# First part of a fused network kernel: the mixer's first weights ahead of the ninth modulation chunk, later chunks set wider, spatial half 0 ahead of half 1

## The reference, cut to what matters

```
for i in range(2):
    m = (silu(c) @ w_mod[i] + b_mod[i]).reshape(6, 1024)       # shifts, scales, gates
    h = x * (1 + s1) + sh1
    mix = chunk_mlp(h, ...) if i == 0 else gla_mixer(h, ...)
    x = layer_norm(DN_ALPHA * x + g1 * mix, ln_g[i, 0], ln_b[i, 0])
    x = layer_norm(DN_ALPHA * x + g2 * peer_ffn(x * (1 + s2) + sh2, ...), ...)

chunk_mlp:  u, v = split(gelu(h @ w_in));  v = layer_norm(v)
            s = W_s @ v (8 heads of 128 channels, over 128 positions) + b_s
            return (u * s) @ w_out
peer_ffn:   q = h @ w_q;  scores = q @ keys;  16 picks for each of 8 heads and row,
            out = sum_k weight_k * gelu(u_table[pick] . h) * v_table[pick]
```

## Time and profile before

| | |
|---|---|
| Three runs | 3691.73, 3691.20, 3690.06 us; median 3691.2 |
| Span of the profiled execution | 3684.9 us |
| Median less that span | 6.3 us |
| TensorE clock granted over the span | 0.972 |
| PE, DVE, ACT, POOL busy | 88%, 68%, 48%, 23% |
| DMA read from HBM | 1159.79 MB, 315 GB/s over the span |

### The profile page before, as it was taken

The page is one execution under the profiler, slowest core; times in us unless marked ns, Lnnn a source line. Parts: engine busy times, 40 slices in busy tenths (PEclk is TensorE's granted clock), DMA queues, the critical chain, the costliest instruction groups (busy, mean ns, idle before and its releaser), DMA issues. The chain is left out here.

```text
span 3684.9 us, 38027 instructions
## 1 busy us (share of the span) xinstructions
PE 3244.8 (88%) x12780; PEld 2023.3 (55%) x12780; DVE 2523.6 (68%) x5106; ACT 1769.7 (48%) x3833; POOL 863.8 (23%) x778
## 2 busy tenths in 40 slices
PE   6878888887798889888887878789999999999998
PEld 3444444442354434446322222279878988988896
DVE  2577778867777787657677677567665657666655
ACT  2334445444554565554444444355464545555453
POOL 0024444444443444410444444300000000000000
PEclk8989999999999999999999999999999999999999
DMA  9979999999999999972999999956655655565553
GB/s 398 373 292 418 418 419 405 419 418 416 418 392 417 419 420 418 419 276 93 410 421 421 421 419 420 418 177 182 184 184 166 186 176 173 166 185 197 157 188 131
DMA packets 280468, 1163.47 MB, mean 316 GB/s; under 512 B 31144, under 2 KB 33704, under 8 KB 175824
## 3 DMA queue, kind: packets, MB, share of 16 engines
q0 software_dynamic: 110592, 805.36, 52.8%
q1 hardware_dynamic: 169296, 355.45, 29.1%
q10 hardware_dynamic: 384, 0.23, 0.0%
HBM read 1159.79 MB, written 1.15 MB: 315 GB/s over the span
## 5 line engine op out<-in xcount | busy, mean ns | idle before, releaser
L86 PE MATMUL psum<-rows,diag 128*128 128x512 f32 x3072 | 1491.5, 622 | 315.9 <-ACT diag L2164 315.0
L2120 DVE CUSTOM_DVE_ANT_0 rows<-rows,h 128x1024 f32<-128x1024 f32 x768 | 938.9, 1224 | 495.9 <-DMA rows<-in_p_uv,place 493.7
L86 PEld LDWEIGHTS psum<-rows,diag 128*128 128x128 f32 x3072 | 559.2, 194 | 1160.8 <-ACT diag L2164 665.8
L2016 POOL DMA_INDIRECT rows<-in_p_uv,place x768 | 859.8, 1120 | 1416.5 <-PE psum L86 1113.8
L2864 DVE TENSOR_TENSOR weights_low<-landing,weights_high 128x1024 fp32r<-128x1024 f32 x400 | 487.0, 1222 | 369.1 <-ACT weights_high L2811 368.0
L2811 ACT CAST weights_high<-landing 128x1024 fp32r<-128x1024 f32 x400 | 417.7, 1049 | 544.9 <-PE psum L86 362.8
L2151 ACT ACTIVATE acted<-dots 128x1 f32<-128x1 f32 x768 | 155.2, 202 | 927.4 <-DVE dots L2120 925.6
L86 PE MATMUL psum<-weights_high,hT_high 128*128 128x512 f32 x832 | 352.9, 424 | 14.5 <-DVE h L694 6.8
L2164 ACT ACTIVATE diag<-ident,weight 128x128 f32<-128x128 f32 x768 | 308.5, 402 | 70.4 <-ACT weight L2157 0.4
L86 PE MATMUL psum<-weights_high,hT_low 128*128 128x512 f32 x832 | 325.8, 392 | 0.0
L86 PE MATMUL psum<-weights_low,hT_high 128*128 128x512 f32 x832 | 325.7, 391 | 0.0
(11 more groups left out here) (431 smaller groups left out, 3875.0 us busy)
## 6 DMA issues: line engine op xcount, KB each, us to landing
landing<-in_w_in SPq DMA_DIRECT2D x192, 512.0 KB, 3.9
landing<-in_w_ff SPq DMA_DIRECT2D x128, 512.0 KB, 4.3
landing<-in_w_mod SPq DMA_DIRECT2D x48, 1024.0 KB, 8.7
landing<-in_a_w_in SPq DMA_DIRECT2D x64, 256.0 KB, 7.4
landing<-in_w_br SPq DMA_DIRECT2D x32, 512.0 KB, 4.3
rows<-in_p_uv,place POOLq DMA_INDIRECT x768, 15.3
lat_landing<-in_b_w_in SPq DMA_DIRECT2D x48, 256.0 KB, 7.4
landing<-in_a_w_out SPq DMA_DIRECT2D x32, 256.0 KB, 7.5
```

Source lines behind the costliest of these rows:

```text
L86: return k.nc.tensor.matmul(out, lhsT, rhs, start=first, stop=last)
L2016: k.nc.gpsimd.indirect_dma_start(rows[:, n % ROW_RING, :], None, k.given["p_uv"], bass.IndirectOffsetOnAxis(place[:, g % 4, c:c + 1], 0))\
L2120: V.tensor_tensor_reduce(u, u, token, 1.0, 0.0, ALU.mult, ALU.add, dots[:, g % 4, c:c + 1]).then_inc(dots_done, 1)
```

## The change

The chunks of the modulation lose the even spacing of 3.5 slots. The mixer's first four blocks are asked for at slot -10, ahead of chunk 8. Rows for v's norm, `ws` and the layer norm are asked for four blocks later. Spatial half 0 and its turns stand 8 slots earlier, half 1 5.5 and 3 slots earlier, blocks 32 to 39 3 to 5 slots and 40 to 47 3 slots earlier. The last store of modulation rows stands at slot 152, and POOL waits for the stores at gather 6 and not at gather 0. No transfer and no arithmetic is added or removed.

```
-AHEAD, MOD_SPREAD = -12, 3.5
+AHEAD = -12
 condition:
-    SLOTS = [AHEAD + n for n in range(DB)] + [1 + MOD_SPREAD * n for n in range(CHUNKS - DB)]
+    SLOTS = [AHEAD + n for n in range(DB)] + [1, 3.5, 6.5] + [11 + 4.1 * n for n in range(13)] \
+        + [66 + 3.4 * n for n in range(12)] + [106 + 1.4 * n for n in range(7)] + [117.5, 121, 122, 126, 130]
 stores:
-            yield SLOTS[DB * q + 7] + 4
+            yield SLOTS[DB * q + 7] + (4 if q + 1 < QUARTERS else 22)
 first_mix:
-    SLOTS = [8 + 2 * n for n in range(32)] + [77, 79, 81, 83, 86, 88, 90, 92] + [94 + 2 * n for n in range(8)] \
+    SLOTS = [8 + 2 * n for n in range(32)] + [72, 74, 76, 78, 83, 85, 87, 89] + [91 + 2 * n for n in range(8)] \
         + [123 + 2 * n for n in range(16)]
-        return SLOTS[p] - 15.5
+        return AHEAD + 2 if s == 0 and p < LANDING else SLOTS[p] - 15.5
 sp_rows:
-        yield load_slot(s, 4) + 0.5
+        yield load_slot(s, 4 if s == 1 else 8) + 0.5
-            yield load_slot(s, 6) + 0.5
+            yield load_slot(s, 10) + 0.5
-            yield load_slot(s, 12) + 0.5
+            yield load_slot(s, 16) + 0.5
-    TURNS_Y = ((0, 0, 72), (1, 0, 72), (0, 1, 82), (1, 1, 82))
+    TURNS_Y = ((0, 0, 64), (1, 0, 64), (0, 1, 79), (1, 1, 79))
-    SPATIAL = ((0, 0, 66), (1, 0, 66), (0, 1, 76), (1, 1, 76))
+    SPATIAL = ((0, 0, 58), (1, 0, 58), (0, 1, 70.5), (1, 1, 70.5))
 wait_rows_free (POOL):
             if n == 0:
                 conditioned.wait_used(pool)
+            if n == 6:
                 conditioned.wait_stored(pool, conditioned.quarters)
```

## The result

The changed kernel took 3697.8 us (median of 11 runs), the kernel before 3690.1 in the 11 runs beside it; ratio 1.0019, 95% interval 1.0011 to 1.0027. Forecast were 3689.4 us and a range to 3696.

What follows compares the result with a forecast made beforehand. Transfers were taken as the bound from the first gather on, so only the first score's time counted: 204.09 - 202.3 = 1.8 us gained, 3691.2 - 1.8 = 3689.4 us, range 3681 to 3696.

Steps and rivals of the forecast that it cites:

- The bound, and that it passes on: From the first gather on, transfers bound the kernel, so an earlier first gather passes through nearly one to one.
- The start: First blocks on PE: early requests let block 0 start near 44.6 us, 6.3 us earlier.
- The list of landings: Chunks and blocks up to the third store land one behind another, chunks 2.49 us apart, a block 0.63 us at 417 GB/s.
- The store wait: SP's wait for the third store: queue drains, SP goes on at 117.0, a DMA hole of about 2.7 us.
- Blocks 36 to 47: On PE, 23.7 us plus some 0.7 for a slow restart; block 47 done at 159.8, 8.3 us earlier.
- The stage behind: Block 47 to block 48: chunks still owed hold block 51 until 180.7; block 48 starts at 183.4, 0.4 us earlier.
- The ring limit: Chunk n + 6 is asked for only when chunk n is used; chunk 41 lands at 163.3, a hole about 3 us.
- The queries: Block 48 to first score: 17.1 us with three chunks fewer, plus 1.8 for PE's slow clock; score at 202.3.
- Sum: First score at 202.3 instead of 204.09, so 1.8 us off the whole: 3689.4 us.
- the store wait decides: Rival, chance 0.13: SP goes on at 123.5 behind the third store, score at 208.8, 4.7 us lost, 3695.9 us.
- full queue: Rival, chance 0.22: no holes before the gathers, DMA at 417 GB/s throughout, 10 us gained, 8 with one hole left, 3682.
- 6.3 us around the span: Whole kernel: the runs stand 6.3 us above the profiled execution's span of 3684.9, giving 3691.2 us before the change.

Runs made afterwards that it cites:

- u_early: The changed kernel with blocks 0 to 3 and the row loads asked for at their old places; 3696.5 us, ratio 1.0020 to the kernel before.
- u_spacing: The changed kernel with the modulation chunks evenly 3.5 slots apart again; 3688.0 us, ratio 0.9998 to the kernel before.
- u_wait: The changed kernel with the loads of g_row and m_rows at slot 74 instead of 65; 3691.4 us, ratio 1.0006 to the kernel before.
- t_only: The changed kernel with blocks 48 to 51 asked for 6.5 slots earlier, ahead of chunks 42 to 47; 3689.9 us, ratio 0.9998 to the kernel before.
- s_store: u_spacing with the third quarter's store at slot 64.5 instead of 57.5; 3691.8 us, ratio 1.0004 to the kernel before.
- c_old: The changed kernel with its context half (among the gathers) in the order of before; 3695.6 us, ratio 1.0018 to the kernel before.

## Why the prediction was wrong, point by point

- **The bound, and that it passes on**: right. The stage of gathers was as long as before to 1 us.
- **The start**: block 0 at 43.5 (44.6 predicted); no worth of it shows in u_early. But block 30 didn't land near 108: ACT got it at 112.59, after waiting 3.06 us for it. The list of landings let DMA run full until the store; DMA moved 320 GB/s at 100 to 120 us, not 417. This is the step that failed first. The gates and block 31's low part followed at about the predicted distance, so block 35 was asked for at 117.2 (112.8) and the store went out at 117.6 (113.5): 4.1 us late. "Block 31 done at 119.2" was wrong too, it was done at 125.7, outside the stated bounds; but PE later stood idle for 6.9 us ahead of block 36, so that delay isn't on the chain. Why block 30 landed late is open: in u_spacing DMA moved 410 to 417 GB/s from 110 to 130 us, and block 35 was asked for no earlier (117.5).
- **The store wait**: the mechanism was there, its size too small: SP paused 5.2 us (3.5) and went on at 122.8, not at 117.0. From there to block 36 it took 22.3 us (18.4), a second mis-sized term: the three row loads were priced at 417 GB/s, and behind them DMA moved 229 and 219 GB/s in the windows 124 to 126 and 126 to 128 us. Together with the late store that makes block 36 9.7 us late (4.1 + 1.7 + 3.9). u_wait shows what the wait cost: 4.8 to 8.2 us at block 36.
- **Blocks 36 to 47**: 25.3 us (24.4 predicted), end at 170.5 (159.8). Everything up to here is 10.7 us.
- **The stage behind**: right in kind. The ring limit, block 51 behind chunks 42 to 47 and the second turn behind block 51 came as described; 26.5 us for 23.6. The prediction so named the debt that t_only then removed, and still forecast a gain, because it had block 47 early enough to pay for it.
- **The queries**: 18.05 us to the first score (18.9), at the slow clock at first, as the earlier trace rows had shown behind an idle time. From the first score to gather 0 it was 12.15 us, as predicted.
- **Sum**: the first score was predicted at 202.3 and came at 214.96: 9.7 + 0.9 + 2.9 - 0.8 = 12.7 us late. The rule "a loss once block 47 ends later than 161.6" held, and so did the sign of being wrong, gather 0 after 217. The rival *the store wait decides* was the case, with 13%. Its time for SP, 123.5, was met within 0.7 us by luck: it put the store at 113.5 with 10.0 us behind it, and the store came 4.1 us later with 5.2 us behind it. Its price of 4.7 us at the score was short by 6.2 through the terms behind it (3.9, 0.9 and 2.9, less 0.7 and 0.8).
- **Two slips** that change nothing: the earlier trace rows has four requests between store and loads, two chunks and two blocks, and not three; and 167.6 + 5 + 1 in *full queue* is 173.6, not 173.9.
- **The range** ended at that rival's price, 3696, so it had no room for the rival being dearer than its price. The 7.7 us measured are just over the 7.4 that the prediction took as the least that tells; slower by more than that had got 0.07.
- **6.3 us around the span**: wrong. The profiled execution of the changed kernel took 3700.57 us at a span of 3698.8; 1.8 us lie around it. If as much lay around the span of before, that execution took 3686.7 us and was 3 to 4 us quicker than the median. The forecast isn't touched by it, since the 6.3 cancel in the sum.
- **The pool wait** at 0 and the context half at 0: right.

## What to carry to other kernels

When transfers are moved behind a stage, look which later transfer stands in line behind them and which engine's queue waits for that one: here 256 KB (block 51) held back some 8 us of PE through ACT's and DVE's order, and asking for it 6.5 slots earlier undid it. Keep a store and the load that waits for it apart by requests that others need. A forecast that lists landings one behind the other is a lower bound: check that someone asks for each of them in time. Before a single part of a change is priced from one profile, look whether the two profiles already differ ahead of it.

## What the runs showed of the hardware

**One wait varies from execution to execution, and the rest follows it.** In the three executions of the changed first half SP stood behind the third store for 5.2, 4.8 and 3.0 us, and asked for `g_row` at 122.84, 121.83 and 120.15. Gather 0 came 104.3, 104.1 and 104.2 us after that, so nearly all of the spread of 2.8 us at gather 0 arose up to this one request. The kernel before stayed within 0.9 us in three executions of its first half.

**A drained queue took long to fill.** `g_row` itself landed 4.3 us after its request at 122.84, sooner than before the change (7.3 us). But DMA was back above 380 GB/s only from 128 us on, and the chunk asked for at 124.17 landed 10.7 us later.

**Behind a drained queue the row loads held DMA to some 250 GB/s.** In s_store they were asked for at 126.3 to 127.6, blocks and chunks only after them. In the windows 128 to 130 and 130 to 132 us, while they were in flight, the DMA engines were busy for a share of 1.05 and 0.96 and moved 248 and 244 GB/s. In c_old it was 270 and 248 GB/s at 122 to 126, with 1.08 and 0.97. Before the change the same loads stood among other requests, and the windows of 118 to 126 us never fell under 398 GB/s. These are loads of one 4 KB row spread to all 128 partitions; whether that or the empty queue makes them slow wasn't tried apart.
